# Layer 1 of a hybrid diffusion backbone: attention taken head by head with its division on GpSimd, and the delta rule's convolution and silu done during the projections

## The reference, cut to what matters

```python
def odd_mixer(h, ...):
    z = jnp.dot(h, P['w_in_cd'][li])
    qkv, gate, beta_logit, decay_logit, qg, kg, vg = split_last(z, ...)
    y_c, delta_state = gated_delta_mixer(qkv, gate, beta_logit, decay_logit, ...)
    q = rms_norm(qg.reshape(B, T, 2, 4, 64), gain); k = rms_norm(kg.reshape(B, T, 2, 64), gain)
    ...                                     # sample: rope on q and k, cached context keys and values in front
    o = gqa_block(q, k, v)                  # per query tile of 128
    y = concatenate([y_c, o])               # then w_out
def gqa_block(qb, k, v):
    s = einsum('bqngd,bknd->bngqk', qb, k) * 64 ** -0.5
    return einsum('bngqk,bknd->bqngd', softmax(s), v)
def gated_delta_mixer(qkv, ...):
    qkv = silu(centred_depthwise_conv(qkv, conv_w))        # 4 taps, 1536 channels
    q, k, v = split_last(qkv, (512, 512, 512)); q, k = l2_normalize(q), l2_normalize(k)
    ...                                     # the chunked recurrence, forward and backward
```

## Time and profile before

| what | value |
|---|---|
| median of 3 runs | 1901.72 us (1900.16 to 1902.12) |
| the profiled execution: its own time | 1902.44 us |
| its span | 1900.6 us |
| PE busy | 1583.7 us, 83% |
| DVE busy | 670.8 us, 35% |
| ACT busy | 445.5 us, 23% |
| POOL busy | 203.8 us, 11% |
| chain that ended last | PE 69%, DVE 15%, DMA 5%, issue 5%, ACT 4% |

### The profile page before, as it was taken

One profiled execution on the slowest core, in us unless ns is written; L12 is line 12 of the kernel. 1 busy time (PEld: TensorE's weight loads), 2 busy tenths in 40 slices (PEclk: granted clock), 3 DMA queues, 4 the chain that ended last, 5 costly groups with the idle time before them and its releaser, 6 DMA issues.

```text
span 1900.6 us, 36972 instructions
## 1 busy us (share of the span) xinstructions
PE 1583.7 (83%) x16252; PEld 1046.0 (55%) x16252; DVE 670.8 (35%) x1293; ACT 445.5 (23%) x722; POOL 203.8 (11%) x202
## 2 busy tenths in 40 slices
PE   5999956779749999978999877687766976999993
PEld 2554424445437776654655455576765545777662
DVE  5134575552350000013142398544454143000003
ACT  4111284441121111103010256421211032111110
POOL 0000000000001111100000000344441000111103
PEclk8999996998869999989999898899988987999996
DMA  9822461454229999982212000000001414999994
GB/s 347 284 89 89 165 244 43 153 204 179 87 76 341 375 388 389 381 279 74 89 44 92 0 1 1 2 2 2 2 2 67 167 58 163 377 372 388 382 392 155
DMA packets 90218, 330.01 MB, mean 174 GB/s; under 512 B 10612, under 2 KB 16360, under 8 KB 81928
## 3 DMA queue, kind: packets, MB, share of 16 engines
q1 hardware_dynamic: 75920, 287.29, 39.6%
q0 software_dynamic: 9168, 32.65, 6.2%
q10 hardware_dynamic: 5032, 8.65, 1.3%
HBM read 303.79 MB, written 24.78 MB: 173 GB/s over the span
## 4 chain that ended last, share of the span: by engine, by line
PE 69%; DVE 15%; DMA 5%; issue 5%; ACT 4%; ACTq 0%; DVEq 0%; POOL 0%; SPq 0%
PE pairs L191 25%; PE pairs L1241 13%; PE pairs L1253 11%; DMA ring<-in_exp_w 3%; PE pairs L1224 2%; DVE sm L1576 1%; PE pairs L417 1%; PE pairs L1871 1%; PE pairs L957 1%; PE pairs L1642 1%; PE pairs L1873 1%; ACT arena L1511 1%; PE pairs L1078 1%; PE pairs L567 1%; DMA ring<-in_w_in_ab 1%
## 5 line engine op out<-in xcount | busy, mean ns | idle before, releaser
L191 PE MATMUL pairs<-hT,ring 128*128 128x128 f32 (+1 forms) x1120 | 305.6, 435 | 2.1 <-ACT hT L315 2.1
L191 PEld LDWEIGHTS pairs<-hT,ring 128*128 128x128 f32 x1120 | 170.0, 192 | 138.5 <-issue 137.1
L315 ACT ACTIVATE arena<-pairs 128x256 f32<-128x256 f32 (+7 forms) x188 | 120.5, 655 | 517.0 <-PE pairs L191 254.4
L191 PE MATMUL pairs<-ring,hT 128*128 128x512 f32 (+1 forms) x448 | 177.4, 557 | 0.0
L1241 PEld LDWEIGHTS pairs<-arena 128*64 128x64 f32 x4096 | 145.6, 139 | 13.8 <-issue 13.7
L1241 PEld LDWEIGHTS pairs<-arena,ring 128*64 128x64 f32 x4096 | 142.8, 137 | 14.1 <-issue 14.1
L1241 PE MATMUL pairs<-arena 128*64 128x80 f32 x4096 | 148.5, 235 | 2.0 <-ACT arena L1274 1.0
L1241 PE MATMUL pairs<-arena,ring 128*64 128x80 f32 x4096 | 145.6, 233 | 1.1 <-issue 1.1
L191 PEld LDWEIGHTS pairs<-ring,hT 128*128 128x128 f32 x448 | 84.8, 190 | 92.2 <-issue 89.1
L1307 DVE TENSOR_SCALAR hT<-pairs,arena 80x512 f32<-80x512 f32 x32 | 23.9, 747 | 273.1 <-ACT hT L1283 273.1
L1253 PE MATMUL pairs<-ring,arena 128*80 128x512 f32 x256 | 112.8, 593 | 1.1 <-DMA ring<-in_exp_w 1.1
(11 more groups left out here) (374 smaller groups left out, 2168.3 us busy)
## 6 DMA issues: line engine op xcount, KB each, us to landing
arena<-in_exp_w SPq DMA_DIRECT2D x48, 2048.0 KB, 19.4
ring<-in_exp_w SPq DMA_DIRECT2D x48, 2048.0 KB, 21.5
ring<-in_w_mod SPq DMA_DIRECT2D x24, 2048.0 KB, 8.1
ring<-in_w_in_ab SPq DMA_DIRECT2D x5, 2048.0 KB, 11.5
ring<-in_w_in_cd SPq DMA_DIRECT2D x5, 2048.0 KB, 7.8
ring<-in_w_out SPq DMA_DIRECT2D x4, 2048.0 KB, 8.6
moe_rows<-arena POOLq DMA_DIRECT2D x2, 2560.0 KB, 16.2
h_rows<-arena POOLq DMA_DIRECT2D x2, 2560.0 KB, 8.4
```

The lines of the kernel that those rows point to most:

```text
L191: last = pe.matmul(out, lhs(k), rhs(k), start=(k == 0), stop=(k == KD - 1))
L315: return eng.activation(dst, src, ACT.Copy) if eng is nc.scalar else eng.tensor_copy(dst, src)
```

## The change

1. **Attention by single heads.** Scores, maximum, exponential and transposes have a unit per head. `("gs", j, e)` stays in pair e; the transposed weights go to pair 2 (e = 0) and pair 3 (e = 1), 640 columns each. The result `("go", j)` goes to columns 768 to 895 of pair 2 (before: pair 3), so its `take` waits until the copy of `("gaT", j+1, 0)` is done. ACT copies head 0's transposed weights, DVE head 1's.
2. **Division on GpSimd.** DVE computes one reciprocal per head (`recip`); GpSimd multiplies (`gqa_pool`, put before `delta_pool`), each head's 640 columns by a column broadcast along them. DVE's two multiplications are gone.
3. **Convolution during the projections.** `delta_conv_dve(v, c)` does the 16 taps of a chunk's four channel tiles right after `read_T(v, 1, c)`; `cv` moves from `hT` (which the projections still read) to the arena. The taps leave the loop.
4. **Silu during the projections.** `delta_silu_act` does all twelve after chunk 2 is read on ACT; they leave `delta_act`.
5. TensorE's wait for all of pair 3 before the loop is gone.

```diff
+        cv = [ar(14232 + UW * i, UW) for i in range(2)]
+        def delta_conv_dve(v, c):
+            ...
+            for ct in range(4 * c, 4 * c + 4):
+                for tap in range(4):
...
+                    if tap == 0:
+                        v.tensor_scalar(y, x, w, None, ALU.mult).then_inc(S("cv_tap"), 1)
+                    else:
+                        v.scalar_tensor_tensor(out=y if tap < 3 else pad[:, ct, 0:UW], in0=x, scalar=w, in1=y,
+                                               op0=ALU.mult, op1=ALU.add).then_inc(S("cv_tap"), 1)
+        def delta_silu_act(act):
+            for ct in range(12):
+                act.wait_ge(S("cv_tap"), 4 * ct + 4)
+                act.activation(pad[:, ct, 0:UW], pad[:, ct, 0:UW], ACT.Silu).then_inc(S("cv_silu"), 1)
# gqa_act
             for j in range(-2, len(GP)):
                 if j + 2 < len(GP):
-                    exps(j + 2)
+                    exps(j + 2, 0)
+                    exps(j + 2, 1)
                 if 0 <= j + 1 < len(GP):
-                    turned(j + 1)
+                    gqa_turned(act, j + 1, 0)
# gqa_dve
+            def recip(j, e):
+                emptied(v, ("gs", j, e))
+                if j >= 4:
+                    v.wait_ge(S("g_norm"), 2 * (j - 4) + e + 1)
+                v.reciprocal(rsum(j, e), psum_of(j, e)).then_inc(S("g_recip"), 1)
+            for j in range(-2, len(GP)):
+                for e in range(2):
+                    if 0 <= j + 1 < len(GP):
+                        recip(j + 1, e)
+                    if j + 2 < len(GP):
+                        maxes(j + 2, e)
+                if 0 <= j + 1 < len(GP):
+                    gqa_turned(v, j + 1, 1)
+                if j >= 0:
+                    result(j)
+        def gqa_pool(g):
+            for j in range(len(GP)):
                 n = T if GP[j][0] < ST else P
                 for e in range(2):
...
+                    g.wait_ge(S("g_recip"), 2 * j + e + 1)
+                    p = gp[j % 2][:, e, 0:n]
+                    g.tensor_tensor(p, p, rsum(j, e).broadcast_to((P, n)), ALU.mult).then_inc(S("g_norm"), 1)
# gqa_pe
+            def turn(j, e):
+                pe.wait_ge(S("g_norm"), 2 * j + e + 1)
+                u = ("gaT", j, e)
+                ps = take(pe, u, 2 + e)
...
-                take(pe, u, 3)
-                emptied(pe, ("gaT", j))
+                res = take(pe, u, 2)[:, 768:896]
+                for e in range(2):
+                    emptied(pe, ("gaT", j, e))
...
-            pe.wait_ge(pair_free[3], units.uses[3])
             for j in range(-2, len(GP)):
-                if j + 2 < len(GP):
-                    scores(j + 2)
-                if 0 <= j + 1 < len(GP):
-                    turn(j + 1)
+                for e in range(2):
+                    if j + 2 < len(GP):
+                        scores(j + 2, e)
+                for e in range(2):
+                    if 0 <= j + 1 < len(GP):
+                        turn(j + 1, e)
                 if j >= 0:
                     rows(j)
# the queues
+                    delta_silu_act(act)              # ACT, after read_T of chunk c in the loop's body's end
+                        delta_conv_dve(v, c)         # DVE, after read_T(v, 1, c, ...)
+            gqa_pool(g)                              # POOL, before delta_pool
```

More of the change, by code:

```diff
@@ L1500, in gqa_act, with exps, gqa_turned @@
                 release(copy(act, gqT[:, g, :], filled(act, ("gqT", g))[:, 0:T]), ("gqT", g))
-            def exps(j):
+            def exps(j, e):
                 n = T if GP[j][0] < ST else P
-                act.wait_ge(S("g_max"), j + 1)
+                act.wait_ge(S("g_max"), 2 * j + e + 1)
                 if j >= 2:
-                    filled(act, ("gaT", j - 2))
+                    filled(act, ("gaT", j - 2, e))
                 if j >= 4:
[L1508 to L1519, removed]
+                    act.wait_ge(S("g_recip"), 2 * (j - 4) + e + 1)
+                u = ("gs", j, e)
+                release(act.activation(gp[j % 2][:, e, 0:n], filled(act, u)[:, 0:n], ACT.Exp, bias=nmax(j, e),
+                                       accum_out=psum_of(j, e)), u)
             for j in range(-2, len(GP)):
                 if j + 2 < len(GP):
-                    exps(j + 2)
+                    exps(j + 2, 0)
+                    exps(j + 2, 1)
                 if 0 <= j + 1 < len(GP):
-                    turned(j + 1)
+                    gqa_turned(act, j + 1, 0)
+        def gqa_turned(eng, j, e):
+            n = T if GP[j][0] < ST else P
+            if j >= 2:
+                filled(eng, ("go", j - 2))
+            u = ("gaT", j, e)
+            release(copy(eng, gaT[j % 2][:, e * n:e * n + n], filled(eng, u)[:, 0:n]), u)
         def decay_dve(v, step):
@@ L1560, in gqa_dve, with maxes @@
         def gqa_dve(v, step):
[L1561 to L1566, removed]
             for n in range(2):
                 release(v.tensor_copy(gkT[:, n, :], filled(v, ("gkT", n))[:, 0:768]), ("gkT", n))
-            def maxes(j):
+            def maxes(j, e):
+                n = T if GP[j][0] < ST else P
+                if j >= 4:
+                    emptied(v, ("gs", j - 4, e))
+                v.tensor_reduce(nmax(j, e), filled(v, ("gs", j, e))[:, 0:n], AX_X, ALU.max, negate=True)\
+                    .then_inc(S("g_max"), 1)
@@ L1632, in gqa_pe, with scores @@
             emptied(pe, ("gkT", 1))
-            def scores(j):
+            def scores(j, e):
                 t, m = GP[j]
-                ps = [take(pe, ("gs", j, e), e) for e in range(2)]
-                q = [gqT[64 * e:64 * e + 64, m, t * P:t * P + P] for e in range(2)]
-                k = [gkT[64 * e:64 * e + 64, m // 2, :] for e in range(2)]
+                u = ("gs", j, e)
+                ps = take(pe, u, e)
+                r = slice(64 * e, 64 * e + 64)
+                q, k = gqT[r, m, t * P:t * P + P], gkT[r, m // 2, :]
                 if t < ST:
[L1641 to L1644, removed]
-                else:
[L1646 to L1657, removed]
+                    pe.matmul(ps[:, 0:512], q, k[:, 0:512], start=True, stop=True)
+                    finish(pe.matmul(ps[:, 512:T], q, k[:, 512:T], start=True, stop=True), u)
+                else:
+                    finish(pe.matmul(ps[:, 0:P], q, k[:, T:768], start=True, stop=True), u)
+            def turn(j, e):
+                pe.wait_ge(S("g_norm"), 2 * j + e + 1)
+                u = ("gaT", j, e)
+                ps = take(pe, u, 2 + e)
+                for b in range(NT if GP[j][0] < ST else 1):
+                    last = pe.transpose(ps[:, b * P:b * P + P], gp[j % 2][:, e, b * P:b * P + P], ident)
                 finish(last, u)
@@ L1953, in delta_act @@
         def delta_act(act, step):
[L1954 to L1959, removed]
             for c in range(4):
```

57 lines of the change are left out of this document (15 added, 42 removed).

## The result

The changed kernel takes **1918.4 us** (median of 5 runs, 1915.6 to 1920.8) against 1901.72 us before (5 runs, 1900.2 to 1905.5): a ratio of **1.0083 (95% interval 1.0066 to 1.0099)**, 0.83% slower. The profiled execution took 1918.4 us, with a span of 1916.6; that is 16.0 us more span than before, where 2.7 us were forecast.

What follows compares the result with a forecast made beforehand. TensorE was taken to bound the projections, a ring of three engines the loop, ACT's line the tail. Loop +5.3 and tail -2.6 gave +2.7, 1905.1 us for the profiled execution, 1904.4 for the median; range 1899 to 1912.

Steps and rivals of the forecast that it cites:

- scores 0 to 2: First rounds of the attention loop: 6.5 us instead of 10.75, -4.3 us.
- pitch: Loop, scores 2 to 16: fourteen pitches of 5.48 us, in all 77.0 us instead of 69.39, +7.6 us.
- clock: Loop: +2.5 us (0 to 5) for two low-clock stretches, at the start and in the short items.
- the short rounds: Loop, scores 16 to the end of the last rows: 16.3 us instead of 16.8, -0.5 us.
- tail: Last rows to the reciprocal: 15.0 us instead of 17.6, -2.6 us (at full clock -4.0).
- Half of 1.28 us is 0.64 us for one head's scores: Start of a loop round: one head's scores take half of both heads' time, so maximum 0 starts at 0.86 us.
- the rival of 1923 us: Loop: POOL sets the pitch, at 2.1 us a multiplication and 6.8 us a round, +18 us; chance 0.05.
- a rival of +10: Loop: clock falls in a third of the fourteen long rounds, pitch there 7.7 us, 1914 us; chance 0.14.
- the forecast case: Whole kernel: the time lies between 1900.5 and 1908.5 us; chance 0.64.
- the heads overlap as meant: Loop: rows don't wait for ACT's copy, pitch 4.5 us, 13.7 us gained, 1891 us; chance 0.05.
- the three signs: Would make the forecast wrong: pitch under 5 us, clock under 0.8, or a POOL operation over 1.5 us.
- the projections' chance: Chance 0.05 that the projections stall where a copy comes 14 us later, up to +5 us, 1909 us.

Runs made afterwards that it cites:

- e2: Changed kernel with head 1's matmuls over the first 512 keys left out from item 4 on; 1930.54 us, one run.
- e3: Changed kernel with ACT's copy of head 0's transposed weights put between its two exponentials; 1914.88 us, one run.
- e5: Changed kernel with rows issued ahead of the next item's transposes, and DVE's result ahead of its copy; 1890.73 us, ratio 0.9933 to the old kernel.
- e4: Changed kernel with the division back on DVE, nothing on GpSimd in the loop, heads still single; 1922.11 us, one run.
- e7: Changed kernel with six matmuls a round, results unread, added in TensorE's gaps before the transposes; 1912.23 us, one run.
- e8: Changed kernel run once more, unaltered; 1915.71 us, one run.
- e1: Old kernel with only the convolution's taps and the silus moved beside the projections, old loop kept; 1894.85 us, ratio 0.9954.
- e6: Old kernel with convolution and silu moved, plus one maximum per head in the loop; 1884.73 us, ratio 0.9901 to the old kernel.

## Why the prediction was wrong

Slower it was, but by 0.83% and not by 0.14%; 1918.4 us lies outside the range of 1899 to 1912. The profiled execution came out 13.3 us over the sum of 1905.1. By the terms of the sum: scores 0 to 2 +2.1, pitch +5.2, clock +4.9, the short rounds +0.5, tail -1.0, start of the loop +2.65, and -1.0 behind the reciprocal. They add up to 13.3. Two terms were mis-sized, the time of one head's scores (item 1) and the clock (item 5); the first is a mistake about what the operation costs, the second a rival given too little.

1. **"Half of 1.28 us is 0.64 us for one head's scores": this step failed.** TensorE does both heads at once, and one head takes as long (the records at 1110.08; e2). The maximum starts at 1.45 and not at 0.86 us, 0.59 late. The rest of the walk was a little too long and gave some back: exponential 1 at 3.10 us (2.65 forecast), ACT's copy at 3.89 (3.42), rows at 4.64 (4.22), scores at 5.88 (5.48). In the earlier trace rows the scores of both heads have one line of x4 with 1.13 us, which doesn't say how the four lie; halving it was my own arithmetic, and the narrow window of before would have shown two of them together (1100.10, 0.70 us, x2). The Trainium skill has the rule, in "TensorEngine Tiling (Array Packing)", under "Key Properties": tiles work independently, and different ones can load weights and multiply in parallel; by its mapping the partitions 0 to 63 and 64 to 127 belong to different tiles. The trace agrees. The change rests on the same error: what it takes apart had been paid only once. The error alone did not make the kernel slower, though: even the forecast's 5.48 us was above 4.83, because of the gate in item 3.
2. **The first rounds, +2.1 us.** Scores 1 came 3.15 us after scores 0, not 2.7: +0.45 by the same error. The next round was 5.40 and not 3.8 us, and there the clock was low (0.74 in the window; ten transposes took 2.39 us, 1.31 at full clock). This part was walked at full clock, with the start's low stretch left to the +2.5, so most of the 1.6 us is the clock again; how much, no run here separates.
3. **The gate was named rightly.** ACT's copy behind both exponentials, through pair 2, opens the rows; e3 moved it and gained 0.21 us a round, e5 got the rows away from it and gained 1.26. e5 also moved DVE's read of the result ahead of its copy, and the two are not told apart.
4. **POOL.** Forecast 1.25 us, measured 1.252, and hidden (e4). The Trainium skill's "GPSIMD Engine Reference", section 3.1, gave an estimate of 1.4 us: the trace is lower. No multiplication took longer than 1.254 us, so the rival of 1923 us falls. The margin was smaller than forecast, 0.2 us (e3) and not 0.4: the second multiplication started 2.42 us after the scores, not 1.89, since its reciprocal stands on DVE behind the late first maximum.
5. **The clock: this term of the sum failed too.** I allowed +2.5 us, for low stretches at the start and in the short items only, and gave 0.14 to a rival of +10; it was 7.4 in the fourteen long rounds, for which the sum had nothing. One low stretch cost 1.5 to 1.6 us there, where I took 1.2. The low level came again and again in the long rounds. With part of the idle time filled (e7), or only the shortest piece of it gone (e3), it came no more in the long rounds after the first ones; with the idle time in one piece (e4) or head 1's long scores gone (e2), it came oftener. Each of these is one execution, and the cause of a single fall stays open. This part is larger than the forecast case allowed, and smaller than the rival.
6. **Projections.** Nothing stalls, as forecast. The 48 taps cost what was forecast, 0.55 + 2.74 us a channel tile (3.28). The +2.65 us at the start of the loop are not a stall: 1.9 of them were there at 891.6 us already, ahead of the first moved tap (966 us), where the two kernels' work is the same. 1.2 of these come from the first 32 matmuls of the projections, 16.70 us and not 15.54, at a granted clock of 0.82 between 874 and 892 us where before had 0.90. The other 0.75 are a low stretch between 1072 and 1075.5 us (0.55, where before had 1.00). In e8 the same kernel started its loop at 1078.24 us, so the term belongs to the execution and not to the change.
7. **Tail.** -3.6 us, between the forecast of -2.6 and the -4.0 named for full clock; the granted clock was 0.87, where it was 0.79. DVE's eight reads are in fact what is late next (1197.62 for 6.07 us, then the square). They end 7.5 us after the last rows, where the walk had 8.6, and from the square to the reciprocal it is 6.4 us as forecast.
8. **The rival "the heads overlap as meant"** needed rows that don't wait for the copy, and 4.5 us a round. e5 is that rival, at 4.62 us and 1890.7 us (1891 forecast for it; so close by luck, since fourteen rounds of 4.62 are 1.7 us more than of 4.5, and the clock and the tail gave it back). The diff had the order that excludes it.
9. **The short rounds, +0.5 us.** As long as before (16.77 us) although the taps are gone. e1, with the taps gone and the heads together, takes 13.89 at the same granted clock (0.85): taking the heads apart costs 2.9 us here too.
10. **The signs.** None of the three signs that were to refute the account came (a pitch under 5 us, a clock under 0.8 in the loop, a POOL operation over 1.5 us), and yet the time lay outside the range. The sign that did miss is the pitch, 5.88 us and not 5.4 to 5.6.
11. **Slips in the working.** The line through the two rows of POOL gives 1.19 us for 640 columns, not 1.22. The bounds of the hand-over give 5.38 to 5.61 us, not 5.35 to 5.65. With half of the projections' chance, slower comes to 0.475, not 0.45. None of them moves the forecast.

## What to carry to other kernels

Before a pair of operations is taken apart to hand over the first half sooner, read in the trace when the first half ends: on TensorE, work on different row halves may already run together, and then the half takes the time of the whole. Splitting the reader was worth it (one maximum per head, -0.6 us a round, e6); of the scores there was nothing to split (e2). When an order is written by hand, work can wait for a small copy that it doesn't read, only because both use one buffer: rows waited for the copy of the next item's weights in pair 2. Issue what needs nothing of that copy ahead of it (e5), before making anything faster.

## What the hardware showed unexpectedly

- **Two fp32 matmuls of 64 rows on different partition halves overlap.** Two of 512 columns start together and take 0.7 us; each head's second follows 0.53 us later, with or without the other head.
- **With less work for TensorE the loop was slower.** e2's had fewer matmuls than after's and its loop took 9.7 us more (granted clock 0.77 against 0.89); e7's had more, and it took 6.5 us less (0.96). Both are one execution each; after and e8 agree within 0.2 us.
- **The low level of 1.2 GHz comes partly at other rounds in each of the two executions traced of one kernel**, but four times in both (behind scores 2, 7, 9 and 14 in after, 5, 7, 12 and 14 in e8). The spread of the times doesn't tell it: the runs of after lie within 5.2 us, those of e5 within 1.0, and those of e6, whose long rounds are as regular as e5's, within 4.7.
